# Where the scan layers' softplus runs: GpSimd's stepwise chain or VectorE's fused one

## The reference, cut to what matters

```
z, xbc, dt = jnp.split(xn @ w_in, [SSD_D_INNER, SSD_D_INNER + SSD_CONV_DIM], axis=-1)
xbc, new_buf = causal_dwconv(xbc, conv_buf, conv_w, conv_b)
xbc = jax.nn.silu(xbc)
dt = jax.nn.softplus(dt + dt_bias)
A = -jnp.exp(a_log)
y, new_state = ssd_scan(xs, dt, A, B, C, ssm_state)
```

## Time and profile before

| | |
|---|---|
| median of 3 runs | 2030.44 us (2025.73 to 2032.26) |
| profiled execution | 2029.18 us, span 2027.5 us, mean granted TensorE clock 0.943 |
| busy, share of span | TensorE 90%, VectorE 66%, ScalarE 47%, GpSimd 24% |
| GpSimd's part of the softplus | two chains (layers 0 and 3), 71.6 to 101.5 us and 1494.2 to 1524.2 us |
| VectorE's part of it | L1714 0.28 us and L1716 1.79 us, once in each of the two layers |

### The profile page before, as it was taken

The page is one execution under the profiler, slowest core; times in us unless marked ns, Lnnn a source line. Parts: engine busy times, 40 slices in busy tenths (PEclk is TensorE's granted clock), DMA queues, the critical chain, the costliest instruction groups (busy, mean ns, idle before and its releaser), DMA issues.

```text
span 2027.5 us, 35723 instructions
## 1 busy us (share of the span) xinstructions
PE 1821.3 (90%) x13417; PEld 1659.4 (82%) x13417; DVE 1334.7 (66%) x2466; ACT 946.9 (47%) x1693; POOL 494.1 (24%) x411
## 2 busy tenths in 40 slices
PE   4999989999999318999999859999899998999997
PEld 4898759999999103399999859999889875899996
DVE  5998796555576984265546876554789879555544
ACT  2456664453344771145434454533445666445333
POOL 2500501441120232244211005411140050144111
PEclk9999989999999558999999979999999998899998
DMA  6464493655567797945555507555535449465540
GB/s 182 125 187 139 113 273 111 211 183 170 166 214 235 264 376 282 352 151 187 166 166 158 178 4 246 177 185 166 155 120 174 138 116 271 126 196 183 183 149 22
DMA packets 317968, 365.02 MB, mean 180 GB/s; under 512 B 7802, under 2 KB 290978, under 8 KB 317750
## 3 DMA queue, kind: packets, MB, share of 16 engines
q1 hardware_dynamic: 296068, 287.41, 45.2%
q0 software_dynamic: 20560, 74.62, 10.0%
q10 hardware_dynamic: 1216, 1.35, 0.2%
HBM read 340.79 MB, written 23.15 MB: 179 GB/s over the span
## 4 chain that ended last, share of the span: by engine, by line
PE 62%; DVE 18%; issue 8%; ACT 5%; POOLq 2%; DVEq 2%; DMA 2%; POOL 1%; ACTq 0%; SPq 0%
PE G L529 17%; PE G L530 17%; PE G L531 17%; DVE wlo L1526 5%; ACT whi L974 3%; DVE sums L1848 2%; DVE pg L1909 2%; DVE pg L1907 2%; PE A L492 1%; DVE xbc L1697 1%; PE A L930 1%; POOLq L1435 1%; PE A L835 1%; PE G L643 1%; PE A L634 1%
## 5 line engine op out<-in xcount | busy, mean ns | idle before, releaser
L1526 DVE TENSOR_TENSOR wlo<-raw,whi 128x2048 fp32r<-128x2048 f32 x234 | 547.8, 2341 | 336.7 <-ACT whi L974 336.6
L974 ACT ACTIVATE whi<-raw 128x2048 fp32r<-128x2048 f32 x234 | 448.0, 1914 | 571.9 <-PE G L531 567.7
L529 PE MATMUL G<-xH,whi 128*128 128x264 f32 x2112 | 606.4, 287 | 24.2 <-DVE xL L1587 13.4
L530 PE MATMUL G<-xH,wlo 128*128 128x264 f32 x2112 | 601.0, 285 | 0.0
L531 PE MATMUL G<-xL,whi 128*128 128x264 f32 x2112 | 600.5, 284 | 0.0
L529 PEld LDWEIGHTS G<-xH,whi 128*128 128x128 f32 x2112 | 400.5, 190 | 34.3 <-issue 18.8
L530 PEld LDWEIGHTS G<-xH,wlo 128*128 128x128 f32 x2112 | 400.7, 190 | 0.1
L531 PEld LDWEIGHTS G<-xL,whi 128*128 128x128 f32 x2112 | 398.7, 189 | 0.0
L529 PE MATMUL G<-aH,whi 128*128 128x264 f32 x1024 | 293.6, 287 | 8.5 <-DVE wlo L1526 8.5
L531 PE MATMUL G<-aL,whi 128*128 128x264 f32 x1024 | 292.1, 285 | 0.0
L530 PE MATMUL G<-aH,wlo 128*128 128x264 f32 x1024 | 292.1, 285 | 0.0
(11 more groups left out here) (406 smaller groups left out, 3067.9 us busy)
## 6 DMA issues: line engine op xcount, KB each, us to landing
raw<-in_mlp_w_up SPq DMA_DIRECT2D x64, 1024.0 KB, 5.4
raw<-in_mlp_w_down SPq DMA_DIRECT2D x64, 1024.0 KB, 5.2
raw<-in_ssd_w_in SPq DMA_DIRECT2D x48, 1024.0 KB, 5.4
pg<-in_cache_k POOLq DMA_DIRECT2D x64, 512.0 KB, 5.6
pg<-in_cache_v POOLq DMA_DIRECT2D x40, 512.0 KB, 6.9
raw<-in_ssd_w_out SPq DMA_DIRECT2D x16, 1024.0 KB, 7.5
raw<-in_ple_w_gate SPq DMA_DIRECT2D x16, 1024.0 KB, 5.1
raw<-in_moba_w_qkv SPq DMA_DIRECT2D x12, 1024.0 KB, 5.1
```

Source lines behind the costliest of these rows:

```text
L529: mm(o, whi[u % 2][:, k, w], act_h[:, x, :], start=first, stop=False)
L530: mm(o, wlo[u % 2][:, k, w], act_h[:, x, :], start=False, stop=False)
L974: fn(whi[u % 2][:], raw[(u + 2) % 4][:], ACT.Copy).then_inc(s_hi, 1)
L1526: V.tensor_tensor(wlo[u % 2][:], raw[(u + 2) % 4][:], whi[u % 2][:].bitcast(F32), ALU.subtract).then_inc(s_lo, 1)
```

## The change

GpSimd's 21 instructions and its wait go. VectorE's two instructions of turn u = 2 become a call of `softplus`, which begins with the same two and does all the rest: 15 instructions and the drains between them, after the taps of the third chunk. The wait for `s_dtd` at the start of the z stage goes too.

```
 # GpSimd, ssd
-                pool.wait_ge(s_dtr, q + 1)
-                x, e, t, z, z2, dt = spl["sp0"][:], spl["sp2"][:], spl["sp3"][:], spl["sp4"][:], spl["sp5"][:], hv_["dt"][:]
-                gp.tensor_tensor(z, z, e, ALU.mult)
-                gp.tensor_scalar(x, x, 0.0, None, ALU.max)
-                pool.drain()
-                gp.tensor_tensor(z2, z, z, ALU.mult)
-                pool.drain()
-                gp.tensor_scalar(t, z2, 1.0 / 17, 1.0 / 15, ALU.mult, ALU.add)
-                for k in (13, 11, 9, 7, 5, 3, 1):
-                    pool.drain()
-                    gp.tensor_tensor(t, t, z2, ALU.mult)
-                    pool.drain()
-                    gp.tensor_scalar(t, t, 1.0 / k, None, ALU.add)
...
-                gp.tensor_tensor(dt, t, x, ALU.add).then_inc(s_dtd, 1)
                 pool.wait_ge(s_dt7, q + 1)
 # VectorE, dt_head
                     if is_first(it) and u == 2:
                         dve.wait_ge(s_dt2, q + 1)
-                        V.tensor_scalar(sp[3], sp[2], 2.0, None, ALU.add)
-                        dve.drain()
-                        V.reciprocal(sp[4], sp[3]).then_inc(s_dtr, 1)
+                        softplus(sp[0], sp[2], sp[3], sp[4], sp[5], hv_["dt"][:])
 # VectorE, start of the z stage
-                dve.wait_ge(s_dtd, q + 1)
                 V.tensor_scalar(dA[:], dt[:], dte_["bvec"][:, 0:1], -1.0, ALU.mult, ALU.mult)
```

## The result

The changed kernel took 2040.42 us (median of 4 runs, 2039.36 to 2041.75) against 2029.25 (4 runs, 2025.73 to 2032.26) for the kernel before on the same chip: the ratio is 1.0063, with a 95% interval of 1.0046 to 1.0080. That is 11.2 us slower by the medians, where +9.5 was forecast; the interval, 9 to 16 us, holds both. The profiled execution took 2040.52 us with a span of 2038.9, so profile against profile the span grew by 11.4.

A forecast was written before the change was run, and what follows sets the result against it. TensorE was taken as the bound, waiting for VectorE's low halves beside GpSimd's softplus. Added steps 6.1 less contention 3.2 a layer gave +5.9 us, the clock 3.6: +9.5, median 2039.9 us, range 2033 to 2046.

The forecast's parts named there:

- The block is on the path: xbc stage: VectorE's added instructions stand ahead of chunk 5's low half, each added microsecond delays chunk 5; 6.1 us a layer.
- The added drain: VectorE's softplus block: each drain between dependent steps was priced at 0.07 us.
- The cheap-steps rival: VectorE's block: steps cost what the 128x8 steps cost, 3.1 us a layer; 2033.8 us, or 2030.2 without the clock; chance 0.07.
- the errata figure of the Trainium skill: VectorE's two-input steps at 0.335 us instead of 0.42: 0.9 us less a layer, end at 2038.1; the row was preferred.
- The contention goes: xbc stage: without GpSimd's work chunks 5 to 9 start 23.48 us apart instead of 26.66, gaining 3.2 us a layer.
- the 46.99: Layer 0, 100.98 to 147.97: eight chunks taken as TensorE's own pace, 5.87 us a chunk.
- The rival that the long turns would stay: Chunks 5 to 9 stay at 6.67 us without GpSimd, drains lengthening the taps; +15.8 us, 2046.2; chance 0.03.
- The clock falls: TensorE's 7.5 us pause ahead of chunk 5 drops its clock in both layers; 1.8 us a layer, 3.6 in all.
- the 45%: TensorE at the lower clock: 17 matmuls where 31 went in 3.40 us, so 45% of low time is lost.
- the 4.0 that was chosen: Low-clock time in us assumed behind chunk 5's pause in each layer, from a range of 3.4 to 6.0.
- The rule of the Trainium skill that was weighed: Waits between matmul bursts drop TensorE's clock and each burst starts low; by it both layers pay, sum +9.5 us.
- The rival of the later pauses: Behind layer 0, three low-clock stretches (1.5 us each) don't recur, 4.6 us come back; +4.9 us, 2035.3; chance 0.12.

The follow-up runs named there:

- E5: Changed kernel with the polynomial terms 17, 15, 13 and 11 left out, four fused steps fewer in the block; ratio 1.0036 to the kernel before.
- E1: Changed kernel with no polynomial on either engine, dt set to 1/(e + 2); ratio 0.9968 to the kernel before, median 2021.59 us against 2029.56.
- E2: Changed kernel plus GpSimd's old 21 instructions behind VectorE's last step, into a tile nobody reads; ratio 1.0079 to the kernel before, 2042.91 us.
- E6: Changed kernel with 56 extra TensorE matmuls between chunks 4 and 5, into a bank nobody reads; ratio 1.0033 to the kernel before.
- E3: Changed kernel with 44 extra TensorE matmuls between chunks 4 and 5, into a bank nobody reads; ratio 1.0040 to the kernel before.
- E4: Changed kernel with the thirteen steps spread, one at the end of each of turns 3 to 15; ratio 0.9987 to the kernel before, median 2025.53 us.
- E8: Changed kernel with ScalarE's logarithm and one VectorE instruction in place of the polynomial; ratio 0.9959 to the kernel before, median 2019.86 us.

## Why the prediction held

**The block is on the path, instruction by instruction.** 6.1 us a layer were forecast; 6.4 and 6.5 were measured between the low halves of chunks 4 and 5 (13.9 and 14.0 against 7.5). The added drain was put at 0.07 and is 0.07 to 0.08 (72.76 to 76.23 for seven steps), and 0.2 us stand between the last step and raw_out as "issue". E5 takes away four steps and gets back four times 0.50 to 0.52. The cheap-steps rival (0.24 each) and the errata figure of the Trainium skill ("VectorE: DVE Perf Modes", section on the TRN2 errata, an estimate of 0.335 us for one, from a row that the same section calls too low for a single operation) are both excluded by 0.42 in the timeline.

**The contention goes.** 3.2 us were forecast, 3.7 measured (E1 against before). The mechanism was right; the term was half a microsecond small because TensorE's own pace was read too slow. Chunk 9 was taken for the last that waits, but chunk 10 still starts right behind its low half, which ends at 106.94 in the kernel before:

```profile
104.66 2.28 DVE L1526 TENSOR_TENSOR wlo<-raw,whi 128x2048 fp32r<-128x2048 f32 x1
...
107.00 0.39 PE L529 MATMUL G<-xH,whi 128*128 128x264 f32 x1
```

So chunk 9 takes 6.02 us (100.98 to 107.00) and lies in the 46.99 from which 5.87 was worked out; undisturbed a chunk takes 5.80. Four chunks at 5.80 would have given 3.5 us, and chunk 9 has the 0.2 that are missing from 3.7. The rival that the long turns would stay falls with E1 and E2. The Trainium skill ("SBUF — State Buffer", section on the two separate sides) says that a VectorE instruction with two SBUF inputs and a GpSimd one that reads SBUF exclude each other for a whole instruction. The trace agrees in part: the six taps grow from 2.79 to 3.93 us while the low half, which has two SBUF inputs too, stays at 2.28 in nearly every turn (E2 has one of 2.55); there it is GpSimd that takes longer. In E2, GpSimd's product L1391 begins at 99.12 behind a low half that began at 98.78, and takes 2.54 us, where it takes 0.83 in the kernel before, so the two engines meet not only at semaphores:

```profile
98.11 0.86 POOL L1389 TENSOR_SCALAR sp<-sp 32x264 f32<-32x264 f32 x1 [0.16 <-issue]
99.12 2.54 POOL L1391 TENSOR_TENSOR sp<-sp,sp 32x264 f32<-32x264 f32 x1
101.81 0.88 POOL L1393 TENSOR_SCALAR sp<-sp 32x264 f32<-32x264 f32 x1 [0.16 <-issue]
```

**The clock falls.** 1.8 us a layer were forecast; E6 against the changed kernel gives 1.5 and 2.4, and the table's rows give 0.44 us lost for each us at the lower level (1.5 of 3.4, 2.3 of 5.2, 2.8 of 6.3, taken over E1's 70.0), as the 45% said. What a single fall costs depends on when in the pause it comes: 3.1 to 6.3 us of the low time lay behind the pause, so the 4.0 that was chosen is a middle and no law. The rule of the Trainium skill that was weighed ("TensorE: Matmul & The Clock Gate", section on HAM oscillation) held in every pause of 2.4 us and more that the changed kernels made in this stage, with one difference: behind the 2.4 us of E3 chunk 5 began at the full clock and lost it 1.3 us later. The waits in that section's example are of 3 to 5 us, so the falls behind shorter pauses in the earlier trace rows, which the prediction counted for the rule, are not what it describes.

**The sum.** 6.4 - 3.7 + 1.5 in layer 0 and 6.5 - 3.7 + 2.3 in layer 3 make 9.3, against 9.5 forecast; the block was 0.3 to 0.4 us a layer small and the contention 0.5, with opposite signs, and the two falls of the clock, 1.5 and 2.3, have the forecast 1.8 between them. That the sum agrees better than its terms is luck. (In the prediction's sum two times 2.9 is 5.8 and not 5.9, which changes nothing.) The remaining difference from 11.4 (span) is not explained by the stage: the stretches outside vary by 7 and 4 us among kernels that are equal there (E4 aside). The rival of the later pauses was half seen: the lower clock behind the pauses at 1041 and 1932 did not recur at the same places, yet the time outside grew. Between the two stages the changed kernel has less time at the lower clock than the kernel before, 180.9 us against 184.3 in the trace, and takes 1.5 us more, so the clock doesn't explain that part; behind the second stage it has 47.2 against 44.5 and takes 1.1 more, which the price above would cover. No experiment followed it up, and where the 2.2 come from stays open.

**Off in the details.** The wait ahead of chunk 5 was to be 7.5 us and was 6.7 and 6.9. In layer 0 chunk 4 ended later (73.6 instead of 72.9); in layer 3 the wait before had been 0.4, and the prediction took layer 0's 1.4 for both. The release of the first z chunk was expected near 152.7 and came at 151.74, by the contention term and the shorter fall, and because chunk 4's low half was there 0.4 us earlier (66.35 instead of 66.75).

## What to carry to other kernels

Work that stands in no chain of waits can still be on the path through another engine that it slows, and work that adds nothing to an engine's busy share can be on it through its place: price a moved step by what is queued behind it, not by the engines' shares. If it must go to an engine that is just ahead of the bound, put it in small pieces, or give it to an engine whose slack is longer than the piece (E8). Compare a turn with its piece with the bound's own: E4's 5.85 us against 5.80 used up the lead, and part of the price came only in the next stage, so the yardstick has to reach past that. A pause that a step opens in the bound engine can cost twice, itself and the clock behind it.

## What the hardware did that was not expected

A remainder of 2.4 us of pause was followed by the lower clock and one of 1.4 us was not (E3), so filling most of a pause can bring nothing at all. How long the clock stayed low behind a pause did not follow the pause's length: 3.4 us behind 6.7, 5.2 behind 6.9, 6.3 behind 5.8, 3.4 behind 4.8. The low stretch itself was 6.8 us in the first three, and the pause hid more or less of it. And the logarithm's two table loads, 2.56 us in a turn of 5.8, cost TensorE no wait, since only half a microsecond of them came out as a late high half.
